# A chunked attention stage reordered: keys before queries, values divided after their matmul, scores in two runs of slots

## What is computed

```python
qkv = h @ w_qkv
q, k, v = jnp.split(qkv, 3, axis=-1)
q = head_rmsnorm(q, q_norm)            # 16 heads of 64
k = head_rmsnorm(k, k_norm)
...
s = einsum('bqhd,bkhd->bhqk', qc, kb) * scale + bias   # relative bias per head
s = where(valid, s, -1e30)
p = softmax(s)
o = einsum('bhqk,bkhd->bqhd', p, vb)
return o @ w_o
```

## Time and profile before

| | before |
|---|---|
| median of 3 runs | 1684.85 us |
| profiled execution, its own time | 1684.69 us |
| span of the profiled execution | 1682.9 us |
| PE busy | 1619.4 us, 96% |
| VectorE busy | 1223.6 us, 73% |
| ScalarE busy | 811.8 us, 48% |
| GpSimd busy | 404.6 us, 24% |
| DMA, share of 16 engines over the span | 52.6% |
| attention stage, first block to the next stage's first | 223.2 to 351.0 us |

### The profile page before, as it was taken

The page is one execution under the profiler, slowest core; times in us unless marked ns, Lnnn a source line. Parts: engine busy times, 40 slices in busy tenths (PEclk is TensorE's granted clock), DMA queues, the critical chain, the costliest instruction groups (busy, mean ns, idle before and its releaser), DMA issues.

```text
span 1682.9 us, 29136 instructions
## 1 busy us (share of the span) xinstructions
PE 1619.4 (96%) x11534; PEld 1487.7 (88%) x11534; DVE 1223.6 (73%) x2115; ACT 811.8 (48%) x1545; POOL 404.6 (24%) x247
## 2 busy tenths in 40 slices
PE   6999998999999999999889999999999999999999
PEld 6999986789999778899889999999999888888887
DVE  6766687676666756566699999999999655555555
ACT  6544544544454555444334454444444444444443
POOL 1111135211111201010167984333343000000000
PEclk9999999999999999999999999999999999999999
DMA  5565654346555644445344554444444555666664
GB/s 182 181 180 185 184 193 162 125 140 189 186 180 179 196 144 131 133 127 176 126 141 150 160 178 152 152 151 155 154 144 144 170 188 187 188 188 188 188 188 137
DMA packets 77478, 277.74 MB, mean 165 GB/s; under 512 B 8600, under 2 KB 9880, under 8 KB 77344
## 3 DMA queue, kind: packets, MB, share of 16 engines
q1 hardware_dynamic: 77344, 275.89, 52.6%
HBM read 274.81 MB, written 1.05 MB: 164 GB/s over the span
## 4 chain that ended last, share of the span: by engine, by line
PE 78%; DVE 16%; issue 3%; ACT 2%; POOL 1%; DMA 0%; SPq 0%; DVEq 0%; ACTq 0%; POOLq 0%
PE ps L835 77%; DVE BIG L1296 3%; DVE WL L355 2%; DVE HL L1299 1%; DVE BIG L1721 1%; ACT WH L481 1%; DVE SQN L1296 1%; DVE BIG L1716 1%; DVE BIG L1719 1%; DVE BIG L1714 1%; DVE BIG L1717 1%; DVE XT L1296 1%; DVE BIG L1753 1%; DVE BIG L1759 1%; POOL NR L406 1%
## 5 line engine op out<-in xcount | busy, mean ns | idle before, releaser
L355 DVE TENSOR_TENSOR WL<-RAW,WH 128x1024 fp32r<-128x1024 f32 x455 | 564.6, 1242 | 233.3 <-ACT WH L481 201.9
L835 PE MATMUL ps<-HH,WH 128*128 128x256 f32 x2048 | 592.8, 289 | 18.0 <-DVE HL L1296 4.5
L835 PE MATMUL ps<-HL,WH 128*128 128x256 f32 x2048 | 581.5, 284 | 0.0
L835 PE MATMUL ps<-HH,WL 128*128 128x256 f32 x2048 | 581.1, 284 | 0.0
L481 ACT ACTIVATE WH<-RAW 128x1024 fp32r<-128x1024 f32 x386 | 405.9, 1053 | 276.4 <-PE ps L835 276.4
L835 PEld LDWEIGHTS ps<-HH,WH 128*128 128x128 f32 x2048 | 394.2, 192 | 24.0 <-issue 9.0
L835 PEld LDWEIGHTS ps<-HL,WH 128*128 128x128 f32 x2048 | 394.7, 193 | 1.0 <-issue 1.0
L835 PEld LDWEIGHTS ps<-HH,WL 128*128 128x128 f32 x2048 | 394.6, 193 | 0.0
L415 POOL CAST WH<-RAW 128x1024 fp32r<-128x1024 f32 x124 | 154.6, 1250 | 414.8 <-PE ps L835 414.7
L835 PE MATMUL ps<-WH,GH 128*128 128x512 f32 x512 | 202.9, 396 | 1.8 <-DVE GL L1296 1.8
L835 PE MATMUL ps<-WL,GH 128*128 128x512 f32 x512 | 202.9, 396 | 0.0
(11 more groups left out here) (229 smaller groups left out, 2341.0 us busy)
## 6 DMA issues: line engine op xcount, KB each, us to landing
RAW<-wall SPq DMA_DIRECT2D x510, 512.0 KB, 3.5
B<-rel SPq DMA_DIRECT2D x4, 768.0 KB, 5.6
DEC<-con SPq DMA_DIRECT2D x4, 384.0 KB, 4.4
XT<-xt SPq DMA_DIRECT2D x4, 256.0 KB, 5.7
out<-XT SPq DMA_DIRECT2D x4, 256.0 KB, 2.1
WIN<-con SPq DMA_DIRECT2D x1, 768.0 KB, 8.7
PAR<-par SPq DMA_DIRECT2D x1, 190.0 KB, 2.4
BIG<-keys SPq DMA_DIRECT2D x1, 128.0 KB, 4.2
```

Source lines behind the costliest of these rows:

```text
L355: ins = eng.tensor_tensor(wl, RAW[:, b % NRAW, :], wh.bitcast(F), ALU.subtract)
L835: return pe.matmul(o, l, r, start=start, stop=stop, skip_group_check=True)
```

## The change

(The diff goes by engine: GpSimd, ScalarE, PE, VectorE.) The four groups come in the order keys low, queries low, keys high, queries high; the keys (groups 0 and 2) are scaled, the queries (1 and 3) copied. GpSimd makes `WH` of only eight blocks of the stage, ScalarE of the others. ScalarE's rescaling of the weights (`weights`) is gone: they are turned as they come from the exponential, two slots after the scores. `values` now holds 128 columns of `PT` stationary and moves 64 columns of values, three matmuls a head, so that tokens are on partitions; VectorE divides there (`values_normed`), PE turns the result back (`values_turned`, four transposes for four heads), and the split is made in four passes of 512 columns. The scores come after slots 10, 11, 13, 14 and after 19, 20, 22, 23; groups 2 and 3 are both turned after slot 17. PE gets waits on `s_pt` 8 (`group_turned(2)`), `s_exp` (`turn`) and `s_an`.

```diff
-    for g in (0, 2, 1, 3):
+    for g in (2, 0, 3, 1):
         names.extend(("qk", 4 * g + k) for k in range(4))
...
+HIGH_ATT = (13, 14, 16, 17, 22, 23, 25, 26)
...
-    return b in SECOND or ATT + 5 <= b < ENTRY[3] or b - MIX in HIGH_MIX or UP + ROUTED + 4 <= b < WP
+    return b in SECOND or b - ATT in HIGH_ATT or b - MIX in HIGH_MIX or UP + ROUTED + 4 <= b < WP
...
-SCALED = {1: 0, 3: 1, 4: 2, 5: 3}
+SCALED = {0: 0, 2: 1, 4: 2, 5: 3}
...
-SCO_SLOT = {12: 0, 13: 1, 15: 2, 16: 3, 19: 4, 20: 5, 22: 6, 23: 7}
-PV_SLOT = {20: (0, 1), 21: (2, 3), 24: (4, 5), 26: (6,), 27: (7,)}
+SCO_SLOT = {10: 0, 11: 1, 13: 2, 14: 3, 19: 4, 20: 5, 22: 6, 23: 7}
+
+PV_SLOT = {20: 0, 21: 1, 24: 2, 26: 3}
+VT_SLOT = {21: 0, 22: 1, 25: 2, 27: 3}
...
-                high(ATT + n + 2)
-                if n == 5:
+                if n in (5, 9, 13, 17):
+                    group_power(n // 4 - 1)
+                if n == 10:
                     power(2)
-                if n in (5, 8, 13, 16):
-                    group_power({5: 0, 8: 1, 13: 2, 16: 3}[n])
+                if high_on_pool(ATT + n + 2):
+                    high(ATT + n + 2)
...
             for n in range(3, 31):
-                if n in (4, 8, 12, 16):
-                    group_squares(n // 4 - 1, ASQ)
-                if n in (7, 12, 14, 19):
-                    g = {7: 0, 12: 1, 14: 2, 19: 3}[n]
...
+                if n in (9, 10, 18):
+                    for g in {9: (0,), 10: (1,), 18: (2, 3)}[n]:
...
-                if n - 4 in SCO_SLOT:
-                    weights_copied(SCO_SLOT[n - 4])
+                if n - 3 in SCO_SLOT:
+                    weights_copied(SCO_SLOT[n - 3])
+                if n in (4, 12):
+                    group_squares(n // 4 - 1, ASQ)
                 if not high_on_pool(ATT + n + 2):
                     high(ATT + n + 2)
-                if n in (4, 12):
+                if n in (8, 16):
+                    act.wait_ge(s_blk, ATT + NAT_LAST[n // 4 - 1] + 1)
                     group_copied(n // 4 - 1)
-                for m in PV_SLOT.get(n - 1, ()):
-                    values_high(m)
-                if n - 2 in SCO_SLOT:
-                    weights(SCO_SLOT[n - 2])
+                    group_squares(n // 4 - 1, ASQ)
+                if n - 1 in VT_SLOT:
+                    values_high(VT_SLOT[n - 1])
                 if n - 1 in SCO_SLOT:
                     exps(SCO_SLOT[n - 1])
...
             def turn(m):
-                pe.wait_ge(s_prob, 4 * m + 4)
-                if m:
+                pe.wait_ge(s_exp, 4 * m + 4)
+                if m == 4:
+                    pe.wait_ge(s_nev, 6)
+                elif m:
                     pe.wait_ge(s_pt, 2 * m)
...
-                    mm(o[r, c:c + T], VN[:, 0, 64 * h:64 * h + 64], PT[:, h, 0:T], True, False)
-                    ins = mm(o[r, c + 128:c + T], VN[:, 1, 64 * h:64 * h + 64], PT[:, h, T:384], False, True)
+                    mm(o[:, c:c + 64], PT[:, h, 0:128], v0, True, True)
+                    mm(o[:, c + 128:c + 192], PT[:, h, 128:T], v0, True, False)
+                    ins = mm(o[:, c + 128:c + 192], PT[:, h, T:384], v1, False, True)
                 ins.then_inc(s_pv, 1)
+
+            def values_turned(g):
+
+                pe.wait_ge(s_an, g + 1)
+                for i in range(4):
+                    ins = pe.transpose(bank[PV_BANK[g]][:, c128(i)], AN[:, g % 2, c128(i)], IDENT)
+                ins.then_inc(s_at, 1)
...
                     if n == 8:
                         pe.wait_ge(s_nsq, 2)
+                        pe.wait_ge(s_nsc, 2)
+                    elif n == 12:
+                        pe.wait_ge(s_nsq, 4)
                         pe.wait_ge(s_nq, 2)
...
-                    if n % 4 == 0:
-                        pe.wait_ge(s_nev, 6 if n == 16 else 8)
+                    if n == 16:
+                        pe.wait_ge(s_nsc, 4)
+                    elif n == 20:
+                        pe.wait_ge(s_nev, 8)
...
-                if n in (6, 11, 13, 18):
-                    group_turned({6: 0, 11: 1, 13: 2, 18: 3}[n], ANAT)
-                if n - 3 in SCO_SLOT:
-                    turn(SCO_SLOT[n - 3])
+                if n in (8, 9, 17):
+                    for g in {8: (0,), 9: (1,), 17: (2, 3)}[n]:
+                        group_turned(g, ANAT)
                 if n in SCO_SLOT:
                     scores(SCO_SLOT[n])
...
+                if n - 2 in SCO_SLOT:
+                    turn(SCO_SLOT[n - 2])
+                if n in VT_SLOT:
+                    values_turned(VT_SLOT[n])
+                if n in PV_SLOT:
+                    values(2 * PV_SLOT[n])
+                    values(2 * PV_SLOT[n] + 1)
...
             for n in range(3, 31):
+                if n in VT_SLOT:
+                    values_normed(VT_SLOT[n])
                 if n - 1 in SCO_SLOT:
                     biased(SCO_SLOT[n - 1])
                     maxima(SCO_SLOT[n - 1])
...
-                if n in (5, 8, 13, 16):
-                    group_mean({5: 0, 8: 1, 13: 2, 16: 3}[n], ASQ)
...
+                if n in (5, 9, 13, 17):
+                    group_mean(n // 4 - 1, ASQ)
+                if n in (7, 14):
+                    g = 0 if n == 7 else 2
+                    group_root(g)
+                    if g == 2:
+                        dve.wait_ge(s_nt, 2)
+                    group_scaled(g, ANAT, natural_banks(g))
+                if n in (10, 18):
+                    group_root((n - 6) // 4, 0.125)
+                if n - 1 in VT_SLOT:
+                    values_low(VT_SLOT[n - 1])
                 low_if_mine(ATT + n + 2)
-                if n == 6:
+                if n == 11:
                     norm_root(2)
```

More of the change, by code:

```diff
@@ L327, in build @@
             "s_em", "s_nsq", "s_nq", "s_nred", "s_nms", "s_npw", "s_niv", "s_nsc", "s_nt", "s_nev"))
-        s_mb, s_sco, s_bia, s_max, s_neg, s_exp, s_rec, s_prob, s_ptr, s_pt, s_pv, s_ah, s_al = (sem(n) for n in (
-            "s_mb", "s_sco", "s_bia", "s_max", "s_neg", "s_exp", "s_rec", "s_prob", "s_ptr", "s_pt", "s_pv", "s_ah", "s_al"))
+        s_mb, s_sco, s_bia, s_max, s_neg, s_exp, s_rec, s_ptr, s_pt, s_pv, s_an, s_at, s_ah, s_al = (sem(n) for n in (
+            "s_mb", "s_sco", "s_bia", "s_max", "s_neg", "s_exp", "s_rec", "s_ptr", "s_pt", "s_pv", "s_an", "s_at", "s_ah",
+            "s_al"))
         s_z, s_zc, s_zb, s_zx, s_zl, s_zn, s_zs, s_zt, s_za, s_ze, s_zv, s_sbh, s_sbl = (sem(n) for n in (
@@ L587, in group_copied @@
                 for t_ in range(2):
-                    if g:
-                        act.wait_ge(s_nt, 2)
-                    act.activation(ANAT[:, 0, t_, :], bank[NAT_BANK[g][t_]][:, :], ACT.Copy).then_inc(s_nq, 1)
+                    if g == 3:
+                        act.wait_ge(s_nt, 4)
+                    act.activation(ANAT[:, 1, t_, :], bank[NAT_BANK[g][t_]][:, :], ACT.Copy).then_inc(s_nq, 1)
             def group_taken(g, dst, gain):
@@ L614, in weights_copied, with values_high @@
                     act.activation(PT[:, 2 * m + a, :], bank[PTR_BANK[a]][:, 0:384], ACT.Copy).then_inc(s_pt, 1)
[L616 to L620, removed]
[L621 to L632 removed]
+            def values_high(g):
+                act.wait_ge(s_at, g + 1)
+                act.activation(AH[:, 2 * g:2 * g + 2, :].rearrange("p k t -> p (k t)"), bank[PV_BANK[g]][:, :],
+                               ACT.Copy).then_inc(s_ah, 1)
+            for n in range(3, 31):
+                if n in (9, 10, 18):
+                    for g in {9: (0,), 10: (1,), 18: (2, 3)}[n]:
+                        group_taken(g, (K, Q)[g % 2][:, 4 * (g // 2):4 * (g // 2) + 4, :], ("attn_k_norm", "attn_q_norm")[g % 2])
                 if n == 20:
@@ L977, in group_turned @@
                     pe.wait_ge(s_ms, 3)
+                elif g == 2:
+                    pe.wait_ge(s_pt, 8)
                 elif g == 4:
@@ L1006, in values @@
             def values(m):
-                o, c = bank[PV_BANK[m // 2]], T * (m % 2)
+                o = bank[PV_BANK[m // 2]]
                 pe.wait_ge(s_pt, 2 * m + 2)
@@ L1498, in reciprocals, with values_normed, values_low @@
                 dve.reciprocal(RC[:, 4 * m:4 * m + 4], SE[:, 4 * m:4 * m + 4]).then_inc(s_rec, 1)
-            def values_low(m):
-                dve.wait_ge(s_ah, 2 * (m // 2) + 2)
-                tt(AL[:, m, :], bank[PV_BANK[m // 2]][:, T * (m % 2):T * (m % 2) + T], AH[:, m, :].bitcast(F), ALU.subtract).then_inc(s_al, 1)
+            def values_normed(g):
+                dve.wait_ge(s_pv, 2 * g + 2)
+                dve.wait_ge(s_rec, 2 * g + 2)
+                if g >= 2:
+                    dve.wait_ge(s_at, g - 1)
+                tt(heads(AN[:, g % 2, :]), heads(bank[PV_BANK[g]][:, :]), RC[:, 8 * g:8 * g + 8].unsqueeze(2).to_broadcast(
+                    [128, 8, 64]), ALU.mult).then_inc(s_an, 1)
+            def values_low(g):
+                dve.wait_ge(s_ah, g + 1)
```

(2 more changed lines are left out.)

43 lines of the change are left out of this document (13 added, 30 removed).

## The result

| | before | after |
|---|---|---|
| median (7 runs each, one chip) | 1685.08 us | 1680.19 us (1678.37 to 1680.96) |
| ratio, 95% interval | | 0.9965 [0.9956, 0.9975] |
| profiled execution: own time, span | 1684.69, 1682.9 us | 1679.36, 1677.6 us |
| attention stage (first block to the next stage's first) | 127.8 us | 123.4 us |
| PE from slot 5 to slot 28 | 101.7 us | 97.9 us |

A forecast was written before the change was run, and what follows sets the result against it. PE's attention stage was taken as the bound, with waits of 10.9 us for `WL` and `ANAT` and 1.3 of clock. Slot 28 7.7 us earlier less new waits 5.5 gave 2.2 us: 1682.6 us, range 1679.4 to 1686.2.

The forecast's parts named there:

- the case given most weight: Whole kernel: time within the 0.2% (3.4 us) that a measurement can't tell from no change; chance 0.64.
- PE's own work: PE, slots 5 to 28 without waits: blocks 66.4, inserted steps 16.1, `values` 10.0, `values_turned` 2.0, sum 94.5 us.
- a turn of six transposes 0.75: PE in the attention stage: each of eight turns keeps its old price of 0.75 us.
- Rival (c): PE's `values`: 128-column loads not hidden, step 0.13 to 0.16, 1685.0 to 1687.9 us, gain gone at 0.128; chance 0.1.
- The start of slot 5: Slot 5 starts 0.4 us earlier, at 237.2, as the wait of 0.31 before it goes.
- The step that failed: GpSimd against VectorE: group 2's power starts first, at 268.6, and holds `low(15)` until 271.5.
- the 2.6 us before the scores after slot 14: PE: scores(3) wait 2.6 us for `biased(2)`, queued on VectorE behind the held `low(15)`.
- the 0.25 at slot 19: PE: slot 19 waits 0.25 us because power 3 holds `low(19)` until 291.25.
- The 2.1 before turn(3): PE: turn(3) waits 2.1 us for a bank, as ScalarE copies turn(2) only behind pair 3's exponentials.
- Rival (b): Power doesn't hold `low`; casts hit group 2's root, waits 4.1, gain 3.6, 1681.2 us; 1679.2 without collision; chance 0.3 together.
- I take no clock loss: PE's clock: no new wait is longer than the 2.79 us after which the clock stayed full, so 0 lost.
- New waits: PE in the attention stage: 0.2 + 2.6 + 2.1 + 0.35 + 0.25 = 5.5 us.

The follow-up runs named there:

- the powers made twice: Changed kernel with every GpSimd power of the stage's four groups made twice, the first into an unused tensor: 1687.99 us, ratio 1.0008.
- split alone: Kernel before with only the casts divided: GpSimd casts eight blocks of the attention stage, ScalarE the others; rest as before: 1674.2 us, ratio 0.9928.
- casts all on GpSimd: Changed kernel with all casts of blocks 5 to 31 of the stage on GpSimd again, none on ScalarE: 1691.45 us, ratio 1.0028.
- turn first: Changed kernel with a pair's turn ahead of the next scores in slots that have both: 1681.46 us, ratio 0.9969.
- the kernel of late turns with the old values: Changed kernel with old values, exponentials ahead of the previous pair's rescaling, first-run turns after slots 13, 14, 17, 18, six blocks cast on GpSimd: 1676.33 us, ratio 0.994.
- the copy first: Changed kernel with ScalarE's copy to `PT` of pair 2 moved ahead of the exponentials of pair 3: 1679.09 us, ratio 0.9955.

## Why the prediction was wrong

The predicted time and its range were near (1682.6, 1679.4 to 1686.2, for 1680.2), but the case given most weight, no change that can be told, isn't what came: the kernel is faster by 0.35%. By its steps:

- **PE's own work.** Slots 5 to 28 without waits: 94.5 forecast; measured 97.85 less 0.31, 2.23 and 1.6, 93.7. `values` took 10.5 where the text had 10.0 (9.6 to 10.8), turning back 1.5 where it had 2.0 (1.6 to 2.4), together the 12.0 forecast. A step of 64 moving columns is 0.108 to 0.112, the upper of the two bounds. Of the 0.8 missing 0.7 are the turns: "a turn of six transposes 0.75" was read where scores follow; none of the new turns has scores or the old `values` behind it, and they took 0.57 to 0.71, and 0.82 once with the wait of 0.31 behind it. The trace of before had this price (0.57 at 330.41). Rival (c), with a step above 0.128, is excluded.
- **The start of slot 5**, 0.4 earlier by the text, came: it starts 14.44 us after the stage's first block before and 14.00 after. The other 1.05 by which it is early were there when the stage began.
- **The step that failed**: "the power of group 2 starts first, at 268.6, and I take it that `low(15)` then stands until 271.5." The order was right (power at 266.92, `low` at 267.03), the hold was not: `low(15)` ended at 268.26, `biased(2)` began at 268.18, and the 2.6 us before the scores after slot 14 didn't come, nor the 0.25 at slot 19. The 2.1 before turn(3) did come (2.23), by the copy behind the exponentials as forecast. I had seen two rows in which a `low` and something of GpSimd's exclude each other and read them as going both ways for both kinds of instruction. They do for casts. For the power they go one way: a `low` just ahead delays it by 0.9 (3.81), a power that has started doesn't delay the `low`. The text's "no row shows a `low` that wants to start during a power" was true of the rows chosen, not of the trace. Two such pairs stand in later stages of the kernel before, the second beside the very power of the earlier trace rows at 656.48:

```profile
563.64 3.81 POOL L406 TENSOR_TENSOR NR<-NR,NHALF 128x16 f32<-128x16 f32 x1 [16.61 <-DVE NR L1299]
```

```profile
565.33 1.23 DVE L355 TENSOR_TENSOR WL<-RAW,WH 128x1024 fp32r<-128x1024 f32 x1 [0.64 <-ACT WH L481]
...
658.47 1.22 DVE L355 TENSOR_TENSOR WL<-RAW,WH 128x1024 fp32r<-128x1024 f32 x1
```

The first starts 1.69 us into a power, the second 1.99, and both take 1.2. So the trace of before could have settled the step that decided the sum. The Trainium skill, page "SBUF — State Buffer", says what the text took from it: in section "Who interferes with whom" that a VectorE instruction with two SBUF inputs contends with a GpSimd instruction that reads SBUF, and in section "SBUF: two separate sides" that of such a pair the one that starts first blocks the other for the whole instruction. The traces don't agree with the latter for a power that starts first: with the `low` 0.11 and 0.12 us behind it (after, and the powers made twice) as with these two, `low` is as long as ever.

- **Rival (b)** had that mechanism and the same sum, 4.1 us of waits, with casts on the root of group 2 (seen, 1.09 for 0.39) and a wait of 2.35 before turn(3) (2.23 measured). It also had 1.3 at slot 16, of which 0.31 came. The mark given for it, a power of 3.8, didn't show: a power of 2.90 with a free `low` was a third case that the text had not foreseen. Its gain of 3.6 and the 0.8 of PE's work make 4.4, where the stage gained 4.3, but that they meet is luck: waits that it had and that didn't come are replaced by clock.
- **"I take no clock loss"** failed as well: 2.23 us of idle time cost 1.6 of half clock, and so filled (b)'s sum up (0.31, 2.23 and 1.6 are 4.1). The reason given, a wait of 2.79 after which the clock stayed full, was one case taken for a rule.
- **Sum.** New waits 5.5 forecast, 2.5 and 1.6 of clock measured: 1.4 less. PE's work 0.8 less. Those 2.2 are, to 0.1, the difference of the stage's gain (4.3 for 2.2). The forecast was this near by luck in part: at full clock the waits would have been off by 3.0.
- **What the text didn't see** at all is which part makes the gain. It counted the old waits away in one sum and took the whole change as their remedy. One edit of it does that alone, with 2.4 us of waits left; the other parts then add 4.2 and 2.8 us of stage. The forecast's own 5.9 us more of PE work for the values pay for waits that the split had already removed. It took the run to show that: when I summed the split by itself, with the result known, I still left the wait of 5.48 standing and expected 1680.5 to 1682.5, for 1674.2.

What stays open: why the clock fell after 2.23 us here and stayed full after longer waits elsewhere, and why the power lets `low` pass and not the other way round. A power that reads its inputs only at its start would fit both; no run tests that.

## What to carry to other kernels

Split a change of many parts before it is judged as a whole: here one edit of a few lines, which engine casts which blocks, held twice the gain, and the larger restructuring spent half of it. When waits are the loss, ask first which queue stands behind the long instruction (casts in order behind a power), and move that queue's work, before PE is given more to do to allow another order. Two engines' exclusion seen for one pair of instructions in one order is a price for that pair and that order only; the other order may stand in another stage of the same trace, and is worth looking for.

## What was not expected of the hardware

- A power on GpSimd (128x16, 2.90 us) and a `low` on VectorE get in each other's way in one order only: the power takes 3.81 us when the `low` starts just ahead, but a `low` takes 1.23 when it starts 0.11, 1.69 or 1.99 behind the power's start. A cast delays the small passes of the root: 1.09 for 0.39, and 0.38 again with the casts gone.
- The granted clock isn't a matter of the last wait's length alone. It stayed 1.00 after PE had been idle for 2.79 (before), 3.01 (casts all on GpSimd, at 246.56), 2.04 (split alone) and 1.98 (turn first), and fell after 2.23 (after), after 2.57 (powers made twice) and after 1.95 (0.83, in the kernel of late turns with the old values). In the last PE ran at full clock for 1.3 us behind the wait before it fell.
- Six transposes cost PE 0.58 before a block and 0.77 before the 64-row matmuls of scores, in one kernel, 4 us apart.
- Outside the stage one execution differs from the next by more than most of these edits are worth: the span less the stage is 1555.1 us before, 1554.2 after, 1554.5 to 1556.1 in most of the others, and 1557.7 (the copy first) and 1558.5 (the turn first). No cause in the edits is shown for these two, whose profiled executions were the slowest of their kernels', 1.7 and 1.2 us above the median. The stage's own length tells edits of 1 us apart where a single time doesn't.
